# The 24 early chunks of u as three fp32r products, with their parts made by ScalarE, VectorE and GpSimd

## The reference

```python
q = (xc @ w_query).reshape(PEER_CHUNK, PEER_HEADS, D_QUERY)
s1, s2 = einsum(q[..., :HALF_Q], keys1), einsum(q[..., HALF_Q:], keys2)
v1, i1 = lax.top_k(s1, PEER_TOPK)
v2, i2 = lax.top_k(s2, PEER_TOPK)
cand = (v1[..., :, None] + v2[..., None, :]).reshape(...)
sc, ci = lax.top_k(cand, PEER_TOPK)
eid = e1 * N_KEYS + e2
gate = jax.nn.softmax(sc, axis=-1)
act = jax.nn.gelu(jnp.einsum('chkd,cd->chk', exp_u[eid], xc))
out = jnp.einsum('chk,chkd->cd', gate * act, exp_v[eid])
```

## Time and profile before

| | |
|---|---|
| time before, median of 3 runs | 1700.96 us (1700.72 to 1704.38) |
| profiled execution | 1703.2 us, span from first to last instruction 1701.4 us |
| busy in the span | PE 1636.1 us (96%), DVE 1330.6 (78%), ACT 630.8 (37%), POOL 487.3 (29%) |
| mean granted TensorE clock | 0.988 |
| early chunks, L1441 | 384 instructions, 126.1 us in records, in the heads and the last run |
| chunks of three products, L1454 | 3 x 832 instructions, 282.2 + 282.6 + 278.2 us |
| chain that ended last | PE 78% |

### The profile page before, as it was taken

The page is one execution under the profiler, slowest core; times in us unless marked ns, Lnnn a source line. Parts: engine busy times, 40 slices in busy tenths (PEclk is TensorE's granted clock), DMA queues, the critical chain, the costliest instruction groups (busy, mean ns, idle before and its releaser), DMA issues.

```text
span 1701.4 us, 24336 instructions
## 1 busy us (share of the span) xinstructions
PE 1636.1 (96%) x8651; PEld 1386.5 (81%) x8651; DVE 1330.6 (78%) x2713; ACT 630.8 (37%) x1050; POOL 487.3 (29%) x511
## 2 busy tenths in 40 slices
PE   7999988999999999987999999999999999999998
PEld 5777665776777679976999999999999999998886
DVE  5788465357898779976788888888888888889886
ACT  5322545221111158862333333333333333333333
POOL 1000000001323300013444444444444444445520
PEclk9999998999999999998999999999999999999999
DMA  8321822042221237889999999999999999999984
GB/s 284 118 73 62 313 75 96 23 153 64 85 64 50 70 91 224 240 283 307 349 340 350 338 351 349 338 343 354 336 338 353 343 339 344 362 333 356 331 313 140
DMA packets 164428, 411.55 MB, mean 242 GB/s; under 512 B 15503, under 2 KB 76461, under 8 KB 162893
## 3 DMA queue, kind: packets, MB, share of 16 engines
q1 hardware_dynamic: 118229, 242.20, 42.2%
q0 software_dynamic: 46080, 167.79, 26.4%
HBM read 375.34 MB, written 33.24 MB: 240 GB/s over the span
## 4 chain that ended last, share of the span: by engine, by line
PE 78%; DVE 2%; DMA 1%; SPq 1%; ACT 1%; issue 0%; DVEq 0%; ACTq 0%
PE bank L1502 31%; PE bank L1454 25%; PE bank L1441 7%; PE bank L1392 7%; PE bank L1483 3%; PE bank L1353 3%; PE bank L1430 1%; DVE placed L1996 1%; DMA u<-in_uT 1%; SPq L1295 1%; DMA gates_kept<-staged 1%; DVE hot_b L1989 0%; DVE here L1992 0%; PE bank L1340 0%; PE bank L1382 0%; DVE h_low L1973 0%
## 5 line engine op out<-in xcount | busy, mean ns | idle before, releaser
L1502 PE MATMUL bank<-v_parts,p_high 128*128 128x512 f32 x1404 | 433.4, 390 | 1.1 <-DVE p_low L1973 1.1
L1725 POOL DMA_INDIRECT rows<-in_u_rows,row_u x160 | 198.5, 1240 | 397.6 <-DVE dots L2029 213.3
L1502 PEld LDWEIGHTS bank<-v_parts,p_high 128*128 128x128 f32 x1404 | 261.7, 188 | 50.0 <-issue 2.2
L1454 PE MATMUL bank<-h_high,u_high 128*128 128x384 f32 x832 | 282.2, 339 | 13.2 <-DVE u_low L1973 12.5
L1725 POOL DMA_INDIRECT rows<-in_v,row_u x160 | 215.5, 1347 | 237.2 <-DVE y L2039 165.2
L1454 PE MATMUL bank<-h_low,u_high 128*128 128x384 f32 x832 | 282.6, 340 | 0.0
L1454 PE MATMUL bank<-h_high,u_low 128*128 128x384 f32 x832 | 278.2, 334 | 0.0
L1502 PE MATMUL bank<-v_parts,p_low 128*128 128x512 f32 x702 | 273.1, 389 | 0.0
L1973 DVE TENSOR_TENSOR u_low<-u,u_high 128x1024 fp32r<-128x1024 f32 x115 | 140.9, 1225 | 146.4 <-ACT u_high L1605 146.1
L1641 ACT CAST p_high<-gel 128x384 fp32r<-128x384 f32 x128 | 65.8, 514 | 379.8 <-DVE gel L2017 356.4
L1454 PEld LDWEIGHTS bank<-h_high,u_high 128*128 128x128 f32 x832 | 156.6, 188 | 17.4 <-DVE u_low L1973 12.9
(11 more groups left out here) (243 smaller groups left out, 2506.7 us busy)
## 6 DMA issues: line engine op xcount, KB each, us to landing
vv<-in_v SPq DMA_DIRECT2D x117, 512.0 KB, 5.6
u<-in_uT SPq DMA_DIRECT2D x104, 512.0 KB
gate<-gates_kept SPq DMA_DIRECT2D x30, 768.0 KB, 8.5
gates_kept<-staged SPq DMA_DIRECT2D x11, 2048.0 KB, 9.6
early<-in_uT SPq DMA_DIRECT2D x24, 512.0 KB, 3.6
w_in_sb<-in_w_in SPq DMA_DIRECT2D x9, 1024.0 KB, 10.3
wq<-in_w_q SPq DMA_DIRECT2D x16, 512.0 KB, 3.6
ckT<-in_ckT SPq DMA_DIRECT2D x4, 1536.0 KB, 13.1
```

The source lines that it names most:

```text
L1454: ins = pe.matmul(a_ps[par][:, 0:DT], x[:, par, k], y, start=(k == 0 and n == 0), stop=(k == KT - 1 and n == 2))
L1502: ins = pe.matmul(y_ps[2 * (i - 1) + half][:], x[:, b, of], y[:, part], start=(t == 0 and n == 0), stop=(t == NK - 1 and n == 2))
L1725: nc.gpsimd.indirect_dma_start(rows[:, r % ROW_BUFS], None, table, bass.IndirectOffsetOnAxis(ap=row_u[:, s_:s_ + 1], axis=0)).then_inc(fet ...
```

## The change

All 24 early chunks go through `activate`, and `activate_early` is gone. Their high parts are made by ScalarE in the heads (behind the copies of each half of the query) and, from z = 3, in the last run behind the gelu three chunks before. Their low parts are made by VectorE at the start of each head on VectorE (chunks 0 to 15), by VectorE for z = 7 and 8 after head 7, and by GpSimd for z = 3 to 6 (behind the sums of tiles 1 to 4 of head 7) and z = 9 and 10 (behind pick of head 7). u has three buffers in place of four; the third one lies in the last slots of the ring. h_high is rounded ahead of head 0, and h_low is made by GpSimd there. GpSimd's pick of the head before comes ahead of the head's sums. Exp comes behind the gelu of z = 7. `h2T`, `tops` and others change their places, and wo_low takes the place of wo, so VectorE waits for `out_samples` ahead of it.

```diff
-EARLY_BUFS = 4
+EARLY_BUFS = 3
+RUN = sum(IN_HEADS.values()) - IN_HEADS[PH - 1]
+RUN_ON_VECTOR = (0, 1, 2, 7, 8)
...
-        h2T = base("h2T", [P, KT, T])
-        h_low = nc.alloc_sbuf_tensor_at("h_low", [P, KT, T], F32R, offset=at)
+        h_low = base("h_low", [P, KT, DT], F32R)
+        h2T_at = GEL_AT - KT * T * 4
+        h2T = nc.alloc_sbuf_tensor_at("h2T", [P, KT, T], F32, offset=h2T_at)
...
-        wo_low = over("wo_low", [P, KT, D], F32R)
+        wo_low = nc.alloc_sbuf_tensor_at("wo_low", [P, KT, D], F32R, offset=s.wo_at)
...
+        def u_after(q):
+
+            return q - EARLY_BUFS + 1 if q < WHOLE + 2 else q - 1
...
+            def load_u(q):
+                wait(sp, a_done, u_after(q))
+                sp.dma_start(u_piece(q)[0], d.uT[q]).then_inc(u_in[u_place(q)], 16)
...
-            def activate_early(q):
-
-                pe.wait_ge(early_in[q % EARLY_BUFS], 16 * (q // EARLY_BUFS + 1))
...
+            def activate(q, halves=(0, 1)):
                 if 0 in halves:
-                    pe.wait_ge(u_split, q - WHOLE + 1)
+                    if q == 0:
+                        pe.wait_ge(h_split, KT)
+                    if q < 2:
+                        pe.wait_ge(h0s_ready, 2)
+                    if q < RUN:
+                        pe.wait_ge(early_split, q + 1)
+                    elif q < WHOLE and q - RUN in RUN_ON_VECTOR:
+                        pe.wait_ge(early_split, RUN + run_part(q - RUN) + 1)
+                    elif q < WHOLE:
+                        pe.wait_ge(run_split, run_part(q - RUN) + 1)
+                    else:
+                        pe.wait_ge(u_split, q - WHOLE + 1)
                     wait(pe, acted, q - 1)
...
                         nc.scalar.copy(qh[:, b, z * HT:(z + 1) * HT], banks[2 * half + z][:, 0:HT]).then_inc(q_taken, 1)
+                    for q in early_after(n)[half:half + (1 if half == 0 else 2)]:
+                        if q < RUN + EARLY_BUFS:
+                            round_u(q)
...
+            for n in range(PH - 1):
+                head(n)
+                for q in early_after(n):
+                    gelu(q)
+            head(PH - 1)
+            for q in early_after(PH - 1)[:-1]:
+                gelu(q)
+                if q == RUN + 7:
+                    act.wait_ge(shifted, 2)
+                    nc.scalar.activation(tops[:, 0:4], tops[:, 0:4], ACT.Exp)
+                    nc.scalar.activation(tops[:, 4, PACK - 1::PACK], tops[:, 4, PACK - 1::PACK], ACT.Exp).then_inc(gate_exp, 1)
+                if q + EARLY_BUFS < WHOLE:
+                    round_u(q + EARLY_BUFS)
...
+            def split_run(z):
+                x, high, rest = u_piece(RUN + z)
+                pool.wait_ge(u_rounded, RUN + z + 1)
+                nc.gpsimd.tensor_tensor(rest, x, high.bitcast(F32), ALU.subtract).then_inc(run_split, 1)
+
             for n in range(PH):
+                if n:
+                    pick(n - 1)
                 for i in range(tiles_of(n)):
                     sums(n, i)
-                if n:
-                    pick(n - 1)
+                    if n == PH - 1 and i:
+                        split_run(2 + i)
             pick(PH - 1)
+            for z in range(IN_HEADS[PH - 1]):
+                if z >= 2 + TILES and z not in RUN_ON_VECTOR:
+                    split_run(z)
...
+            dve.wait_ge(samples_outed, 1)
             for k in range(KT):
-                if k < 2:
-                    split_cat(0, k)
                 dve.wait_ge(o_rounded, k + 1)
...
                 m = tiles_of(n)
+                for z, q in enumerate(early_after(n)):
+                    if n < PH - 1 or z < EARLY_BUFS:
+                        split_early(q)
...
+            for z in RUN_ON_VECTOR[EARLY_BUFS:]:
+                split_early(RUN + z)
             decode(PH - 1)
...
-                if n == HOTS:
-                    dve.wait_ge(a_done, WHOLE)
-                    split_h()
```

More of the change, by code:

```diff
@@ L1173, in route @@
         slot_turned, slot_taken = sem("slot_turned"), sem("slot_taken")
-        u_in = [sem(f"u_in{b}") for b in range(2)]
+        u_in = [sem(f"u_in{b}") for b in range(EARLY_BUFS)]
         v_in = [sem(f"v_in{b}") for b in range(V_BUFS + 2)]
@@ L1206, in early_after, with u_place, u_load, u_piece @@
             return range(first, first + IN_HEADS.get(n, 0))
+        def u_place(q):
+            return q % 2 if q >= WHOLE else q % EARLY_BUFS
+        def u_load(q):
+            return q // EARLY_BUFS + 1 if q < WHOLE else WHOLE // EARLY_BUFS + (q - WHOLE) // 2 + 1
+        def u_after(q):
+            return q - EARLY_BUFS + 1 if q < WHOLE + 2 else q - 1
+        def u_piece(q):
+            b = u_place(q)
+            return (u[:, b], u_high[:, b], u_low[:, b]) if b < 2 else (u3[:], u3_high[:], u3_low[:])
+        def run_part(z):
+            return sum(y in RUN_ON_VECTOR for y in range(z)) if z in RUN_ON_VECTOR else sum(
+                y not in RUN_ON_VECTOR for y in range(z))
         def early_with(b):
@@ L1584, in gelu, with round_u @@
                 nc.scalar.activation(gel[:, q], a_ps[q % 2][:, 0:DT], ACT.Gelu_apprx_tanh).then_inc(acted, 1)
+            def round_u(q):
+                x, high, _ = u_piece(q)
+                act.wait_ge(u_in[u_place(q)], 16 * u_load(q))
+                nc.scalar.copy(high, x).then_inc(u_rounded, 1)
             act.wait_ge(h_taken, 2 * TILES)
-            for n in range(PH):
-                head(n)
-                for q in early_after(n)[:7]:
-                    gelu(q)
             for k in range(KT):
                 nc.scalar.copy(h_high[:, k], h2T[:, k, P:END]).then_inc(h_rounded, 1)
-            act.wait_ge(shifted, 2)
-            nc.scalar.activation(tops[:, 0:4], tops[:, 0:4], ACT.Exp)
-            nc.scalar.activation(tops[:, 4, PACK - 1::PACK], tops[:, 4, PACK - 1::PACK], ACT.Exp).then_inc(gate_exp, 1)
+            for n in range(PH - 1):
[11 more added lines that the diff above has]
+                    round_u(q + EARLY_BUFS)
             def whole(n):
@@ L1601, in whole @@
                                hot_b[:, n % 2].rearrange("p g k t -> p g t k")).then_inc(hot_made, 1)
-            def round_u(q, par):
-                act.wait_ge(u_in[par], 8 * (q - WHOLE - par) + 16)
-                nc.scalar.copy(u_high[:, par], u[:, par]).then_inc(u_rounded, 1)
-            for q in early_after(PH - 1)[7:-1]:
-                gelu(q)
             whole(0)
@@ L1800, in _, with low, split_early @@
                 nc.vector.tensor_tensor(h0s[:, half], banks[6 + n][:], g2_row[:, half], ALU.mult).then_inc(h0s_ready, 1)
+            def low(part, whole, high, rounded, value):
+                dve.wait_ge(rounded, value)
+                return nc.vector.tensor_tensor(part, whole, high.bitcast(F32), ALU.subtract)
+            def split_early(q):
+                x, high, rest = u_piece(q)
+                low(rest, x, high, u_rounded, q + 1).then_inc(early_split, 1)
             def search(n, i):
@@ L1969, in _, with split_u @@
             counts = spread(count[:].rearrange("p (o k) t -> p o k t", o=1), [P, TB // 2, NK, 2])
-            def low(part, whole, high, rounded, value):
-                dve.wait_ge(rounded, value)
-                return nc.vector.tensor_tensor(part, whole, high.bitcast(F32), ALU.subtract)
-            def split_h():
-                for k in range(KT):
-                    low(h_low[:, k, P:END], h2T[:, k, P:END], h_high[:, k], h_rounded, k + 1).then_inc(h_split, 1)
-            def split_u(q, par):
-                low(u_low[:, par], u[:, par], u_high[:, par], u_rounded, q - WHOLE + 1).then_inc(u_split, 1)
+            def split_u(q):
+                x, high, rest = u_piece(q)
+                low(rest, x, high, u_rounded, q + 1).then_inc(u_split, 1)
             for n in range(BATCHES):
-                if n == HOTS:
-                    dve.wait_ge(a_done, WHOLE)
-                    split_h()
                 if n % (GB // TB) == 2 and n // (GB // TB) in range(1, IN_GATES + 2):
-                    split_u(WHOLE + n // (GB // TB) - 1, (n // (GB // TB) - 1) % 2)
+                    split_u(WHOLE + n // (GB // TB) - 1)
                 wait(dve, hot_made, n - 1)
```

79 lines of the change are left out of this document (34 added, 45 removed).

## The result

The changed kernel took 1692.13 us in the median of 5 runs (1691.70 to 1692.86), the kernel before 1700.96 (5 runs beside it, 1698.83 to 1704.38). The medians differ by 8.8 us. The ratio of the runs is 0.9945 with a 95% interval of 0.9934 to 0.9956, so by it 9.4 us (7.5 to 11.2) were gained. The profiled execution of after has a span of 1691.1 us and took 1692.9; before, the span was 1701.4.

A forecast was written before the change was run, and what follows sets the result against it. TensorE was taken to set the pace, with VectorE hardly behind in five-tile heads. Terms 1.2 - 13.8 + 3.1 + 1.0 - 0.9 - 1.5 = -10.9 us gave a median of 1690 us, range 1681 to 1697.

The forecast's parts named there:

- TensorE's gain: In the heads, 13 early chunks were to take 4.20 us each, 1.06 less than before: -13.8 us.
- Start: Before the heads, VectorE waits for the samples' product because wo_low overwrites wo, so the first split ends later: +1.2 us.
- Heads, ScalarE: In the heads, roundings ahead of the score copies make TensorE wait, 1.8 us over six heads and 1.3 in head 7: +3.1.
- head 4: After five-tile head 3, VectorE's first split in head 4 ends at 4.2 us, where TensorE wants it at 3.3: +1.0, once.
- Heads, VectorE: In four-tile heads, VectorE's work becomes 25.5 us with two more splits and earlier picks, fitting TensorE's new period of 26.8.
- Rival (c): In the heads, pick beside hits and splits holds VectorE, making the kernel slower: +18.9 us, 1709; chance 0.06.
- The last run: Last eleven early chunks: GpSimd's queue, holds and late gates eat nearly all the gain, 57.0 us against 57.95: -0.9.
- Rival (a): The last run keeps TensorE's pace; buffers, holds and the chain to the gates cost nothing: 1680 us; chance 0.18 with near cases.
- Half clock: In the last run, TensorE's wait in the slots' transposes lowers its granted clock afterwards: 1.6 us, charged once.
- Gates: In the gates, h_low leaves VectorE's queue but ScalarE's queue keeps part of the gain: -1.5 us, bounds 0 and 2.4.
- From there to the end everything is moved, not changed.: After the gates, to the kernel's end, work only changes place: no change in time, 0 us.

The follow-up runs named there:

- before_wait: The kernel before, with VectorE waiting for the samples' product ahead of its wo_low instructions; 1702.65 us, ratio 1.0005 to the kernel before.
- pick_behind: The changed kernel with GpSimd's picks behind its sums again in heads 1 to 6; 1695.94 us, ratio 0.9965 to the kernel before.
- z10_vector: The changed kernel with VectorE instead of GpSimd subtracting z = 10, behind the gates' product; 1689.45 us, ratio 0.9928 to the kernel before.
- no_low_parts: The changed kernel without subtractions in chunks 0 to 23, the third product taking u's high part again; 1680.77 us, ratio 0.9878 to the kernel before.
- z7_gpsimd: The changed kernel with GpSimd instead of VectorE subtracting z = 7, ahead of the last picks; 1692.79 us, ratio 0.9948 to the kernel before.
- pad: The changed kernel with gate, staged, v, p and rows moved 5120 bytes to their addresses in the kernel before; 1692.92 us, ratio 0.9951 to it.
- low_pitch: The changed kernel with h_low's old row pitch, which moves x1 and u's buffers to old addresses too; 1691.93 us, ratio 0.9940 to the kernel before.

## Why the prediction was right, point by point

- **TensorE's gain, -13.8.** Held. A chunk takes 4.27 to 4.30 us rather than 4.20 (8.54 and 8.59 a pair), so some 13 x 0.08 = 1.0 us less.
- **Start, +1.2.** The wait came as predicted (1.3 us), its cost did not show in the traces: +0.1. The step took for granted that what is late there stays late. before_wait has the wait alone, with +0.05 up to head 0's chunk: its trace has one spell of half clock less behind it. Whether that was luck of one trace of the kernel before is open.
- **Heads, ScalarE, +3.1, and head 4, +1.0.** The three terms cannot be parted in the sum, but together the heads came out at -10.6 against -9.7, the period at 26.75 against 26.8. TensorE's wait for the third score in head 7 was 1.00 (predicted 1.3), and head 4's wait for its splits was 0.42, with 0.34 in head 5.
- **Heads, VectorE.** The relief of VectorE by the earlier picks was there (cast 0.30, bits 0.19), and pick_behind shows what it is worth. Rival (c), pick beside hits and splits, had a grain of truth: GpSimd's instructions of pick took 0.96 us in the mean, 0.63 before. Most took 0.62, and those that met VectorE's hits or splits up to 3.68. But it was GpSimd that waited and VectorE that went on.
- **The last run, -0.9.** This is the step that was mis-sized: +1.2. The order of events was as written: sums of tile 4 late behind a subtraction (VectorE idle 2.33), a hold by z = 6, z = 7 late by 3.31 (predicted 3.0), half clock behind it, a wait in the transposes of 4.1 (predicted 5.2). A GpSimd subtraction took 2.39 us, not 2.2, well within the bounds. The hold by z = 6 fell on the bits (1.77), not on the cast of keyf that the prediction named: in the earlier trace rows the two casts of 128x80 took 0.38 beside a pick, and 0.38 again here. What was missing is the last hold: the gates' product beside z = 10, 2.96 us in place of 0.90. z10_vector removes it and gains 1.4 us. Two further errors cancelled, which is luck. Counted from the start of the last run the second decode ended 1.3 us late (42.3, predicted 41.0), and the table load of 1.28 us, which the prediction put in front of Exp, was over before Exp's input came (589.76, Exp at 593.14). So Exp ended at 44.4, predicted 44.5. That the subtractions, and nothing else, keep the last run at 59 us is what no_low_parts shows (47.75, predicted 47.2 with nothing late), and z7_gpsimd shows which of the two waits counts. Rival (a) is what that experiment built, at 1680.8 against the 1680 worked out for it. In the working, 4.2(z - 2) + 3.6 + 1.05 is 4.2z - 3.75 and not 4.2z - 3.65, which changes nothing else by more than 0.1 us. And the prediction says that the Trainium skill speaks against this part, while the lock that it quotes from "SBUF — State Buffer", section "SBUF: two separate sides", each engine holding off the other for a whole instruction, is what the part's own holds assume, and the trace has such holds (1.77 us for 0.18, 2.96 for 0.90, 3.68 for 0.62).
- **Half clock, 1.6 once.** There were two spells, at z = 7 and behind the transposes. The first cost nothing (pad); with the second, z = 9 and 10 took 9.53 us, 1.0 more than a pair in the heads. These windows of the changed kernel (columns as in the first windows) show TensorE busy nearly throughout at half speed or little more:

```profile
584.00:586.00 2.00, 2.00 (x8) 2.00 (x8) 0.00 (x0) 0.00 (x0) 2.00 (x4) 0.50 0.04 8
...
598.00:602.00 4.00, 3.85 (x15) 3.85 (x16) 3.90 (x9) 0.00 (x0) 0.00 (x0) 0.58 0.00 0
```

- **Gates, -1.5.** -0.9, and its two parts were not what was written. From the gates' first product to the last copy to `staged`, at whose end SyncE goes on, it took 118.45 us in place of 120.73: 2.3 less, so h_low was worth nearly the whole 2.4, and ScalarE's queue kept next to nothing of it. From there to the first full step it took 44.23 in place of 42.87. This stretch, a store of gates and loads of u, is 42.6 and 42.9 us in the two traces with the kernel before and 43.7 to 44.6 in the other twelve; the prediction left it unchanged, and why it is longer is open.

```profile
740.64 0.61 SPq L1286
...
727.03 0.61 SPq L1304
```

  These are SyncE's marks in the chains, first of the kernel before, then of the changed one.
- **"From there to the end everything is moved, not changed."** Wrong by 1.9 us, in low_pitch's terms: moving h_low and u made a step 8.31 us in place of 8.29. The stretch at the end of the gates, above, belongs here too.

The sum of the misses, -1.1 - 0.9 + 2.1 + 0.6 + 1.9 = +2.6, is the difference between -10.9 and -8.3. The start of the samples' product, 2.0 us earlier for no reason in the prediction, hid most of it in the spans, and with it the time came out 2 us from the forecast: that closeness is in part luck.

## What to carry to other kernels

When a cheaper matmul form asks three other engines for parts, count its price where an in-order queue has something else behind it: here the subtractions cost under 1 us in the heads and 11 us in a run of eleven chunks in a row. Of several waits of TensorE only the one on the chain that ends last is worth removing (the one at z = 7 gave 0.5 us by itself, and more only once the transposes had moved), and where that chain can't be shortened, moving its consumer one chunk later was worth more than any new share-out of the work. A wait of 1 us ahead of a stretch where the clock falls may cost nothing, so its price is to be measured and not read off.

## What was unexpected of the hardware

Which instructions of VectorE GpSimd's subtraction holds depends on their kind. A TENSOR_SCALAR of 128x80 took 1.77 us beside it and 0.18 after it, four TENSOR_TENSOR of 128x128 took 2.96 in place of 0.90, but a TENSOR_REDUCE that ran beside z = 9 took 2.68, hardly more than the 2.57 beside pick. The Trainium skill, "SBUF — State Buffer", section "SBUF: two separate sides", has a VectorE instruction take the lock when it has two inputs in SBUF or runs in a two-port mode; the trace agrees for these. For the casts of keyf the shape decides in these traces, not what GpSimd runs: two of 128x64 took 1.26 beside pick in place of 0.30, while two of 128x80 (five tiles in place of four) took 0.38 beside pick, beside the subtraction, and in no_low_parts with neither beside them.

The other way round, VectorE's own two-input instructions, back to back, hold GpSimd and are hardly slowed themselves: the first instruction of the last pick took 3.68 us and not 0.62, ending behind the last of them, while the ten hits stayed at 2.10 and the two splits took 2.36.

The same products of the same shapes ran 0.2% slower a step (8.31 us in place of 8.29) with an operand at another pitch or place. And behind the same idle stretch of 2.9 to 3.0 us the traces show the clock at its lower level now around 343 us, now around 352, and in the kernel before at both; what decides it is not shown.
